# Head norms with tokens on partitions: small sums, root and reciprocal, spread back by TensorE, instead of a 128x512 root and reciprocal

## The reference

```python
def rms_norm(x, gain):
    xf = x.astype(jnp.float32)
    y = xf * lax.rsqrt(jnp.mean(xf * xf, axis=-1, keepdims=True) + EPS)
    return (y * gain.astype(jnp.float32)).astype(x.dtype)
...
        aq = apply_axial_rope(rms_norm(a_q.reshape(bsz, seq, A_HEADS, A_HEAD_DIM), a_q_norm[l]), cos, sin)
        ak = apply_axial_rope(rms_norm(a_k.reshape(bsz, seq, A_KV_HEADS, A_HEAD_DIM), a_k_norm[l]), cos, sin)
...
        bq = rms_norm(b_q.reshape(bsz, seq, B_HEADS, 2, B_HEAD_DIM), b_q_norm[l])
        bk = rms_norm(b_k.reshape(bsz, seq, B_HEADS, 2, B_HEAD_DIM), b_k_norm[l])
```

## Time and profile before

| | us |
|---|---|
| median of three runs | 1887.93 |
| lowest, highest | 1887.75, 1890.23 |
| span of the profiled execution | 1882.6 |
| PE busy in it | 1712.7 (91%) |
| DVE busy | 1230.0 (65%) |
| ACT busy | 860.1 (46%) |
| POOL busy | 495.1 (26%) |
| mean granted clock of TensorE | 0.94 |

### The profile page before, as it was taken

How to read it: one execution, slowest core, us unless ns; L and a number is a source line. 1 busy time by engine, 2 the same in 40 slices (tenths; PEclk the granted TensorE clock), 3 DMA queues, 4 the chain that set the end, 5 groups by cost and what they waited for, 6 DMA issues and landing times. The chain is left out here.

```text
span 1882.6 us, 35550 instructions
## 1 busy us (share of the span) xinstructions
PE 1712.7 (91%) x13260; PEld 1625.1 (86%) x13260; DVE 1230.0 (65%) x1750; ACT 860.1 (46%) x1250; POOL 495.1 (26%) x511
## 2 busy tenths in 40 slices
PE   5887799999977999999999456999999999789999
PEld 5775799998856999999999435999999998579999
DVE  7677666657786766655557986655555556865553
ACT  3445355533543555444444243544354434435442
POOL 3040333310211433223320002333123311343320
PEclk9987899999986999999999757999999999899999
DMA  6330256644320556656654301566455654235563
GB/s 223 101 112 23 90 170 178 222 161 135 102 67 23 159 179 194 198 164 179 196 200 135 101 1 56 177 182 215 164 168 180 212 179 145 67 101 179 179 214 99
DMA packets 70800, 274.25 MB, mean 146 GB/s; under 512 B 7872, under 2 KB 9024, under 8 KB 70592
## 3 DMA queue, kind: packets, MB, share of 16 engines
q1 hardware_dynamic: 70272, 271.04, 46.3%
q0 software_dynamic: 448, 2.13, 0.3%
HBM read 272.09 MB, written 1.05 MB: 145 GB/s over the span
## 5 line engine op out<-in xcount | busy, mean ns | idle before, releaser
L744 DVE TENSOR_TENSOR wl<-raw,wh 128x1024 fp32r<-128x1024 f32 (+1 forms) x474 | 632.5, 1335 | 299.5 <-ACT wh L504 298.7
L1130 PE MATMUL gb<-hh,wh 128*128 128x256 f32 x2768 | 802.4, 290 | 26.3 <-DVE wl L744 17.0
L1131 PE MATMUL gb<-hl,wh 128*128 128x256 f32 x2768 | 788.6, 285 | 0.0
L1132 PE MATMUL gb<-hh,wl 128*128 128x256 f32 x2768 | 787.9, 285 | 0.0
L504 ACT ACTIVATE wh<-raw 128x1024 fp32r<-128x1024 f32 (+1 forms) x474 | 528.5, 1118 | 343.7 <-PE gb L1132 339.6
L1130 PEld LDWEIGHTS gb<-hh,wh 128*128 128x128 f32 x2768 | 536.6, 194 | 41.6 <-DVE wl L744 17.0
L1131 PEld LDWEIGHTS gb<-hl,wh 128*128 128x128 f32 x2768 | 536.9, 194 | 3.2 <-issue 2.9
L1132 PEld LDWEIGHTS gb<-hh,wl 128*128 128x128 f32 x2768 | 536.6, 194 | 0.0
L1131 PE MATMUL gb<-gul,wh 128*128 128x256 f32 x1056 | 298.7, 283 | 0.0
L1132 PE MATMUL gb<-guh,wl 128*128 128x256 f32 x1056 | 298.3, 282 | 0.0
L1130 PE MATMUL gb<-guh,wh 128*128 128x256 f32 x1056 | 296.5, 281 | 1.8 <-POOL gul L493 1.7
(11 more groups left out here) (190 smaller groups left out, 1666.5 us busy)
## 6 DMA issues: line engine op xcount, KB each, us to landing
raw<-in_wa SPq DMA_DIRECT2D x378, 512.0 KB, 3.6
raw<-in_wb SPq DMA_DIRECT2D x96, 704.0 KB, 4.1
x<-in_x SPq DMA_DIRECT2D x1, 1024.0 KB, 4.9
out_x<-x SPq DMA_DIRECT2D x8, 128.0 KB, 3.1
row<-in_row POOLq DMA_DIRECT2D x1, 836.0 KB, 10.6
tab<-in_bias SPq DMA_DIRECT2D x3, 256.0 KB, 4.4
con<-in_const POOLq DMA_DIRECT2D x1, 544.0 KB, 7.7
tab<-in_bias SPq DMA_DIRECT2D x1, 512.0 KB, 4.8
```

Of the source, the lines that this page charges most:

```text
L744: nc.vector.tensor_tensor(wl[:, slot, 0:nt * P], raw[:, slot, 0:nt * P], wh[:, slot, 0:nt * P].bitcast(f32), ALU.subtract).then_inc(s_lo, 1)
L1130: nc.tensor.matmul(bank, a, rhs_h(k), start=start and k == 0, stop=False)
L1131: nc.tensor.matmul(bank, a, rhs_l(k), start=False, stop=False)
L1132: last = nc.tensor.matmul(bank, b, rhs_h(k), start=False, stop=stop and k == nt - 1)
```

## The change

The sums are now made with tokens on partitions. For each of the four 128x128 pieces of a group's `sq` (two chunks, two halves of the tokens), PE takes the piece as the stationary operand and streams two columns of `C_BLK`, one per head. The result is 128 tokens by 2 sums; a group has 128x8. ACT takes the root of 128x8 into `small`, DVE the reciprocal of 128x8 in place.

To bring it back to channels on partitions, the item `norm` now has a part for PE: eight matmuls, each with one column of `small` repeated 64 times as the stationary operand and the identity as the moving one, write 64 equal rows of 128 tokens each to `MISC`. The lower and the upper half of the partitions are written by separate matmuls in turn. DVE's multiplication with the gain then reads `MISC` instead of `sq`. Between the reciprocal and that multiplication DVE waits for PE (`qk_spread`).

The table `W` is changed so that `norm` mostly stands one step after `sum`. POOL may square the next group as soon as the sums of the last are made. In the first `mix1` the rotation of group 0 moves ahead of norm 1, and in step 26 `sum` 5 moves ahead of `cout`.

```diff
@@ do (scalar) @@
-                    w = len(gains) * SEQ
+                    w = 4 * len(gains)
                     act.wait_ge(m["qk_sums"], g + 1)
-                    nc.scalar.activation(sq[:, 0:w], MISC[:, 0:w], ACT.Sqrt, bias=eps[:, 0:1], scale=1.0 / d).then_inc(m["qk_sd"], 1)
+                    nc.scalar.activation(small[:, 32:32 + w], MISC[:, 0:w], ACT.Sqrt, bias=eps[:, 0:1],
+                                         scale=1.0 / d).then_inc(m["qk_sd"], 1)
@@ head_norm (vector) @@
+                w = 4 * len(gains)
                 dve.wait_ge(m["qk_sd"], g + 1)
-                w = len(gains) * SEQ
-                link(nc.vector.reciprocal(sq[:, 0:w], sq[:, 0:w]))
+                nc.vector.reciprocal(small[:, 32:32 + w], small[:, 32:32 + w]).then_inc(m["qk_inverse"], 1)
+                dve.wait_ge(m["qk_spread"], g + 1)
                 for k, (name, at0) in enumerate(gains):
                     ins = nc.vector.scalar_tensor_tensor(out=yc(c + k), in0=yc(c + k), scalar=col(name, at0),
-                                                         in1=sq[:, k * SEQ:(k + 1) * SEQ], op0=ALU.mult, op1=ALU.mult)
+                                                         in1=MISC[:, k * SEQ:(k + 1) * SEQ], op0=ALU.mult, op1=ALU.mult)
@@ do (tensor) @@
                 if what == "sum":
-                    w = len(qk_groups(kind, l)[g][1]) * SEQ
                     pe.wait_ge(m["qk_squared"], g + 1)
                     take_misc(m["qk_sd"], g + 1)
-                    nc.tensor.matmul(MISC[:, 0:w], con[:, C_BLK:C_BLK + P], sq[:, 0:w], start=True, stop=True).then_inc(m["qk_sums"], 1)
+                    two = view(con[:, C_BLK:C_BLK + 1], [[64, 2]])
+                    for t in range(2 * len(qk_groups(kind, l)[g][1])):
+                        end = nc.tensor.matmul(MISC[:, 2 * t:2 * t + 2], sq[:, t * P:(t + 1) * P], two, start=True, stop=True)
+                    end.then_inc(m["qk_sums"], 1)
+                elif what == "norm":
+                    pe.wait_ge(m["qk_inverse"], g + 1)
+                    take_misc(m["qk_normed"], g + 1)
+                    for t in range(2 * len(qk_groups(kind, l)[g][1])):
+                        for half in range(2):
+                            inverse = view(small[:, 32 + 2 * t + half:33 + 2 * t + half], [[0, 64]])
+                            end = nc.tensor.matmul(MISC[64 * half:64 * half + 64, t * P:(t + 1) * P], inverse, ident,
+                                                   start=True, stop=True)
+                    end.then_inc(m["qk_spread"], 1)
@@ W, one line of mix1 (the others change alike) @@
-        W = {"mix1": [(1, "sqr", 0), (2, "sum", 0), (2, "norm", 0), (3, "sqr", 1), (4, "sum", 1), (4, "norm", 1),
+        W = {"mix1": [(1, "sqr", 0), (2, "sum", 0), (3, "norm", 0), (3, "sqr", 1), (4, "sum", 1), (4, "rotate", 0),
```

More of the change, by code:

```diff
@@ L221, in build_program @@
         s_eps, s_ini, s_inie = sem("eps_set"), sem("start_values"), sem("start_exps")
-        NAMES = ("qk_squared qk_sums qk_sd qk_normed rotated roped v_transposed v_tokens scores maxima exps "
+        NAMES = ("qk_squared qk_sums qk_sd qk_inverse qk_spread qk_normed rotated roped v_transposed v_tokens scores maxima exps "
                  "probs probs_turned probsT attn_out attn_copied mix_psum mix_sbuf mix_hi mix_lo").split()
@@ L268, in build_program @@
         NL = len(LEVELS)
-        W = {"mix1": [(1, "sqr", 0), (2, "sum", 0), (2, "norm", 0), (3, "sqr", 1), (4, "sum", 1), (4, "norm", 1),
-                      (5, "rotate", 0), (5, "rope", 0), (6, "turn", 0), (7, "rotate", 1), (7, "rope", 1),
+        W = {"mix1": [(1, "sqr", 0), (2, "sum", 0), (3, "norm", 0), (3, "sqr", 1), (4, "sum", 1), (4, "rotate", 0),
+                      (4, "rope", 0), (5, "norm", 1), (6, "turn", 0), (7, "rotate", 1), (7, "rope", 1),
                       (9, "attn", 0), (10, "attn", 1), (11, "attn", 2), (12, "attn", 3), (13, "attn", 4), (13, "gates", 0),
@@ L277, in build_program @@
                       (18, "level", 2), (19, "level", 3), (19, "turn", 3), (20, "level", 4), (20, "turn", 4), (20, "sqr", 2),
-                      (21, "level", 5), (21, "sum", 2), (21, "norm", 2), (22, "level", 6), (22, "sqr", 3), (23, "level", 7),
+                      (21, "level", 5), (21, "sum", 2), (22, "norm", 2), (22, "level", 6), (22, "sqr", 3), (23, "level", 7),
                       (23, "sum", 3), (23, "attn", 6), (23, "norm", 3), (24, "level", 8), (24, "sqr", 4), (25, "sum", 4),
-                      (25, "norm", 4), (25, "attn", 7), (25, "sqr", 5), (26, "cout", 0), (26, "sum", 5), (26, "norm", 5)] +
+                      (25, "attn", 7), (25, "norm", 4), (25, "sqr", 5), (26, "sum", 5), (26, "cout", 0), (26, "norm", 5)] +
                      [(26, "attn", t) for t in range(8, 14)] + [(26, "post", 0)],
@@ L283, in build_program @@
                       (6, "conv", 4), (7, "sig", 3), (7, "conv", 5), (8, "conv", 6), (9, "turn", 0), (9, "conv", 7),
-                      (10, "conv", 8), (11, "sqr", 0), (11, "conv", 9), (12, "sum", 0), (12, "norm", 0), (12, "sqr", 1),
-                      (12, "conv", 10), (13, "attn", 0), (13, "sum", 1), (13, "norm", 1), (13, "sqr", 2), (13, "conv", 11),
-                      (14, "attn", 1), (14, "sum", 2), (14, "norm", 2), (14, "attn", 2), (14, "conv", 12), (14, "attn", 3),
+                      (10, "conv", 8), (11, "sqr", 0), (11, "conv", 9), (12, "sum", 0), (12, "sqr", 1),
+                      (12, "conv", 10), (13, "norm", 0), (13, "attn", 0), (13, "sum", 1), (13, "sqr", 2), (13, "conv", 11),
+                      (14, "attn", 1), (14, "norm", 1), (14, "sum", 2), (14, "attn", 2), (14, "norm", 2), (14, "conv", 12), (14, "attn", 3),
                       (14, "attn", 4), (14, "conv", 13), (14, "attn", 5), (14, "attn", 6), (14, "conv", 14), (14, "attn", 7),
                       (14, "attn", 8), (14, "conv", 15), (14, "attn", 9), (14, "attn", 10), (14, "attn", 11), (14, "ln", 0)],
[L289 to L292, removed]
+             "odd": [(2, "turn", 0), (4, "turn", 1), (5, "sqr", 0), (6, "sum", 0), (7, "norm", 0), (7, "sqr", 1), (8, "sum", 1),
+                     (8, "attn", 0), (9, "norm", 1), (9, "sqr", 2), (9, "attn", 1), (10, "sum", 2),
+                     (10, "attn", 2), (11, "norm", 2), (11, "sqr", 3), (11, "attn", 3), (12, "sum", 3), (12, "attn", 4),
+                     (13, "norm", 3), (13, "attn", 5), (14, "attn", 6), (14, "pool", 0), (15, "attn", 7), (15, "pool", 1), (16, "attn", 8),
                      (16, "pool", 2), (16, "attn", 9), (16, "pool", 3), (16, "attn", 10), (16, "attn", 11)]}
@@ L422, in square @@
                 if g >= 1:
-                    pool.wait_ge(m["qk_normed"], g)
+                    pool.wait_ge(m["qk_sums"], g)
                 nc.gpsimd.tensor_tensor(sq[:, 0:w], yc(c, len(gains)), yc(c, len(gains)), ALU.mult).then_inc(m["qk_squared"], 1)
```

## The result

| | before | changed |
|---|---|---|
| median, us | 1888.39 (4 runs, 1887.75 to 1890.23) | 1934.64 (4 runs, 1933.61 to 1941.13) |
| span of the profiled execution, us | 1882.6 | 1932.9 |

The ratio is 1.0254, with a 95% interval of 1.0237 to 1.0271: the changed kernel is slower by 2.5%. The forecast was 1913.9 with a range of 1894 to 1938. The sign and the range hold; of the 46.3 us between the medians the sum had 26.0. Between the two profiled executions the difference is 50.3 us, because the one of the kernel before was a short one.

What follows compares the result with a forecast made beforehand. PE, busy 91% of the span, was taken as the bound, so DVE savings count only where PE waits. 12.8 + 9.4 - 4.0 + 7.8 = +26.0 us on 1882.6, plus 5.3 around it, gave 1913.9 us, range 1894 to 1938.

Steps and rivals of the forecast that it cites:

- The unit's end: After a gate-up unit, ACT's copy and DVE's subtraction hold whatever follows on DVE until 2.4 us after PE finishes.
- ten places: Norms directly behind a unit's tiles: two per mix1 start, group 2 of each tail, four in odd; 2.7 us idle each.
- rival 1: The spread's two output halves run one after another, 3.9 us in place of 1.9: +54, 1942 us; chance 0.20.
- rival 4: The sums cost more because weights of sq load without overlap: +15, 1929 us; chance 0.07.
- starts of the two mix1: Two new waits and a rotation's wait, 10.85 us, less old idle and low clock: net +6.9 and +5.9, together +12.8.
- their tails: End of each mix1: +0.3 at norm 2, +1.4 at norm 3, then a serial chain from norm 4; +4.7 each, +9.4.
- even: DVE's own stretch: shorter reciprocals and no root waits, against idling for spreads and later scores; net -4.0 us.
- odd: Four norm places cost 22.7 us together, less 14.9 of earlier idle and low clock: net +7.8 us.
- The low clock at a place: After PE idles, the following unit runs at the 1.2 GHz level, a loss of about 1.25 us per place.
- the 14.9 us that I took off: In odd, earlier idle of 2.41, 4.90 and about 0.5 us plus low-clock losses of 3.5 and about 3.6, expected to vanish.
- Rival 2: The clock stays up over the stalls, 8 x 1.25 = 10 us less: 1904 us; chance 0.15.
- Rival 3: DVE is the bound wherever a norm stands, PE finds the reciprocal ready, 23 us off: 1865 us; chance 0.09.

Runs made afterwards that it cites:

- e_inverse_early: Changed kernel with DVE's small reciprocal as its own table item right behind each sum, spread and multiplication unmoved: 1881.63 us, ratio to before 0.9964.
- e_filler: Changed kernel with two useless 512-column fp32 matmuls on PE ahead of each wait for the reciprocal, except in even: 1914.99 us.
- e_cout_early: Changed kernel with the outer projection cout in mix1 moved from between sum 5 and norm 5 to ahead of norm 4: 1925.47 us.

## Why the prediction was right, and where its sum was too small

**The mechanism held, for the most part as written.** The unit's end puts the reciprocal 2.4 us late; PE's waits before L1263 were forecast at 2.6 to 2.8 us in ten places and are 2.58 to 2.86 in those ten. The two waits in each tail were forecast at about 3.8 and are 3.04 and 4.97: 43 us outside `even`, 42 forecast. L804 takes 0.19 us (0.17), the eight sums 0.95 us (0.9), the spread 1.09 (0.95 without its tail, 1.16 with it). e_inverse_early shows that these waits, with the clock that follows them, are the loss: without them the kernel is faster than before. Behind nine of the ten waits the clock fell to 0.50, no later than 2.3 us after the spread's start; behind the one of group 2 in the second `mix1` it stayed at 1.00.

**The sum was little more than half of what came, and that the range holds the result is partly luck.** The measured 1934.64 is 20.7 us above the forecast. The range reaches to 1938 only for the sake of rival 1, whose mechanism is out; the dearest of the others, rival 4, stood at 1929. Piece by piece, from the same points in both traces:

| stretch | forecast | measured |
|---|---|---|
| starts of the two mix1 (to the second rotate) | +6.9, +5.9 | +9.6, +6.2 |
| their middles (to sum 2) | 0, 0 | 0.0, +2.1 |
| their tails (from sum 2 to L1310) | +4.7, +4.7 | +11.2, +11.5 |
| even | -4.0 | -2.3 |
| odd | +7.8 | +13.0 |

**The term that was sized worst is the tail**, 13.3 of the 24 us that are missing between these two traces. The prediction's chain was right in its members and wrong in their clock. From the row of norm 4's spread on: it begins 1.2 us later than forecast; `cout`, priced 3.7 us from the row of the second `mix1` in the earlier trace rows, which ran at clock 1.0, took 7.1 at clock 0.50; the second spread 1.98, not 1.2; and L901 follows the turn by 3.1 us, not 1.4, since the scores between them run at the low clock too. 1.2 + 3.4 + 0.8 + 1.7 = 7.1, and L901 comes 11.7 us later than L899 did, not 4.7 (the difference is 7.0). Unit 24 of the same tail started 2.0 us later, not 1.4, and took 4.96 us. The prediction calls this chain serial; it should have priced it at the low level throughout.

**The low clock at a place was under-priced.** 1.25 us came from a unit that followed the idle time at once. At the four places of the `mix1` starts, spread and unit behind it together took 1.5 us more than at clock 1.00 (the second `mix1` has the spread in 1.09 and the unit in 4.64 instead of 3.1). At the first place of `odd` the clock was low from the spread on: 1.98 instead of 1.09, and the unit still 4.90 instead of 3.1, which is 2.7 us. The other spreads of `odd` ran in 1.09, 1.22 and 1.09.

**`odd` and `even`.** `odd`'s four waits are 2.82 to 2.86 us, the forecast ones, and e_inverse_early takes all of +13.0 back. Of the other 5 us above the forecast, 1.4 are the first place just named; the rest isn't placed, and the 14.9 us that I took off cannot be checked one by one. In `even` the chain of waits came out 1.7 us longer than worked out.

**The rivals.** Rival 1 (halves one after another, 1942) is out: 1.98 us at the low clock, not 3.9. The Trainium skill's TensorEngine Tiling, section Key Properties, has tiles run independently; the measured 1.09 against 1.58 us agrees that the halves gain by alternating, but by 1.45 times, not 2. Rival 1's price was wrong as well: it put 28 us on the missing overlap, and taking the overlap away cost 4.0 us without the waits and, in a single run, 1.5 us with them. Rival 2 (the clock stays up) is out: it stayed up behind one of the ten waits; e_filler shows what filling them gives. Rival 4 (dearer sums) is out: 0.95 us against 1.02 to 1.13. Rival 3 named a condition, "if PE finds the reciprocal ready each time", and e_inverse_early meets it outside `even`: 1881.6, not 1865. Its spreads keep PE busy for 28.7 us and its multiplications hold PE for 27.0 us, which used up what DVE's freedom gave, except in `even` (-5.2 us); that is read from one trace and not tested apart. Only with `cout` at the high clock as well does it come near, 1869.3.

## What to carry to other kernels

A short instruction that a busy engine waits for belongs ahead of that queue's long items, in the step in which its input is ready; here 0.2 us of DVE moved up by one step was worth 53 us, while the 60 us of DVE work that the change removed were worth 8 us once that was done (1889.4 to 1881.6). When a change puts a wait in front of PE, price the work behind the wait at the low clock, the whole chain of it, and not only from a row that happened to run at the high one. And give an operation that another engine waits for its own entry in the table, so that it can be moved without the rest.

## What the runs showed that I had not expected

- Work of no use can make the kernel faster: 35.2 us of filler matmuls took 19.7 us off, because the granted clock behind them stayed up (1.00 instead of 0.59 over one unit in `odd`).
- Matmuls alternating between the two halves of the output partitions gain only in part: 16 records of 128 columns in 1.09 us alternating and 1.58 us apart at clock 1.00, 1.98 and 2.88 at 0.50.
- The length of a small matmul block doesn't predict its worth: 9.6 us more in the spreads cost 4.0 us, and 14 us more cost 1.5 us in a single run. That the clock of what follows made up the rest is likely and not shown.
- The same 32 records of `cout` took 3.79 us in the first `mix1` and 7.09 in the second of one and the same kernel (e_cout_early). Which of the short pauses ahead of it decides is open.
